# Sample attention: another order of the dilated mixer's far rows on the partitions

## What is computed

```python
DILATED_PATTERNS = ((128, 1), (512, 4), (2048, 16))
for window, dil in DILATED_PATTERNS:
    idx = n_buf + jnp.arange(T)[:, None] - dil * jnp.arange(window // dil + 1)[None, :]
    valid, idx = (idx >= 0), jnp.maximum(idx, 0)
    kg, vg = k_all[:, idx], v_all[:, idx]
    s = einsum('bthe,btjhe->bthj', q, kg) * scale
    p, lse = softmax_stats(s, valid);  o = einsum('bthj,btjhe->bthe', p, vg)
return merge_by_denominator(parts)
```

## Time and profile before

| | |
|---|---|
| Median of the runs | 2409.5 us |
| Profiled execution | 2408.45 us; 2406.9 us from its first to its last instruction |
| Granted TensorE clock, mean | 0.904 |
| TensorE busy (matmul) | 2074.7 us, 86% of the span |
| VectorE, ScalarE, GpSimd busy | 575.7, 379.6, 99.5 us |
| DMA | 537.21 MB in 287292 packets, mean 223 GB/s |
| Sample attention | from 254 to 637 us of the span |

### The profile page before, as it was taken

How to read it: one execution, slowest core, us unless ns; L and a number is a source line. 1 busy time by engine, 2 the same in 40 slices (tenths; PEclk the granted TensorE clock), 3 DMA queues, 4 the chain that set the end, 5 groups by cost and what they waited for, 6 DMA issues and landing times. The chain is left out here.

```text
span 2406.9 us, 52735 instructions
## 1 busy us (share of the span) xinstructions
PE 2074.7 (86%) x22761; PEld 1414.9 (59%) x22761; DVE 575.7 (24%) x1206; ACT 379.6 (16%) x924; POOL 99.5 (4%) x184
## 2 busy tenths in 40 slices
PE   6979488788789999889765786899999999999975
PEld 4755354355367777657443684566876666667643
DVE  2023254253210000112236623211112111111103
ACT  2014132232110000112001320210111011011101
POOL 0000111212100000000000000000000000000001
PEclk9989689889999999996886757899999999999987
DMA  7339699999843230554401011779897879889795
GB/s 269 105 133 337 205 258 321 282 290 321 282 161 140 87 141 1 184 164 169 125 16 30 12 36 57 286 281 347 331 350 285 321 280 376 327 336 406 294 409 174
DMA packets 287292, 537.21 MB, mean 223 GB/s; under 512 B 30021, under 2 KB 80130, under 8 KB 287068
## 3 DMA queue, kind: packets, MB, share of 16 engines
q1 hardware_dynamic: 273894, 492.37, 58.4%
q0 software_dynamic: 12960, 41.43, 5.0%
q10 hardware_dynamic: 214, 0.13, 0.0%
HBM read 520.44 MB, written 13.44 MB: 222 GB/s over the span
## 5 line engine op out<-in xcount | busy, mean ns | idle before, releaser
L2312 PE MATMUL PS<-moe_ring,moe_X 128*32 128x256 f32 (+1 forms) x5376 | 295.0, 369 | 20.8 <-DMA moe_ring<-in_moe_w 15.5
L415 PE MATMUL PS<-H,w_ring 128*128 128x320 f32 (+1 forms) x1008 | 282.0, 443 | 33.0 <-DMA w_ring<-in_w_in_odd 20.1
L2332 PE MATMUL PS<-moe_ring,moe_HT 128*32 128x256 f32 x4224 | 261.6, 382 | 3.6 <-issue 2.3
L415 PEld LDWEIGHTS PS<-H,w_ring 128*128 128x128 f32 (+1 forms) x1008 | 194.2, 194 | 117.2 <-DMA w_ring<-in_w_in_odd 20.4
L2312 PEld LDWEIGHTS PS<-moe_ring,moe_X 128*32 128x32 f32 x5376 | 185.5, 112 | 117.2 <-issue 20.2
L2312 PE MATMUL PS<-moe_ring,H 128*32 128x256 f32 (+1 forms) x3840 | 204.7, 362 | 4.7 <-issue 4.7
L1145 PE MATMUL PS<-H,ffn_ring 128*128 128x320 f32 x704 | 191.7, 436 | 3.5 <-ACT H L240 3.5
L833 PE MATMUL PS<-ident,KV 128*128 128x128 f32 x832 | 123.3, 313 | 72.9 <-DMA KV<-in_cache_win_kv 25.2
L2332 PEld LDWEIGHTS PS<-moe_ring,moe_HT 128*32 128x32 f32 x4224 | 148.0, 111 | 63.8 <-issue 7.1
L2312 PEld LDWEIGHTS PS<-moe_ring,H 128*32 128x32 f32 x3840 | 133.4, 110 | 65.2 <-issue 6.6
L1145 PEld LDWEIGHTS PS<-H,ffn_ring 128*128 128x128 f32 x704 | 134.9, 192 | 60.1 <-issue 4.8
(11 more groups left out here) (463 smaller groups left out, 1841.7 us busy)
## 6 DMA issues: line engine op xcount, KB each, us to landing
moe_ring<-in_moe_w SPq DMA_DIRECT2D x168, 1024.0 KB, 10.3
moe_ring<-in_moe_w SPq DMA_DIRECT2D x40, 2048.0 KB, 15.9
ada_ring<-in_ada_w SPq DMA_DIRECT2D x24, 2048.0 KB, 15.2
KV<-in_cache_win_kv SPq DMA_DIRECT2D x128, 256.0 KB, 9.0
KV<-in_cache_moba_kv POOLq DMA_DIRECT2D x128, 256.0 KB, 6.5
KV<-in_cache_moba_kv SPq DMA_DIRECT2D x128, 256.0 KB, 8.5
ffn_ring<-in_ffn_w SPq DMA_DIRECT2D x14, 2048.0 KB, 12.8
moe_ring<-in_moe_w SPq DMA_DIRECT2D x32, 512.0 KB, 8.4
```

What stands on the lines that cost most here:

```text
L415: last = pe.matmul(PS[0:width, banks[g % B], 0:TOK], RING[:, n % R, k, m:m + width], rhs[:, k, :], start=(k == 0), stop=(k == KT - 1))
L2312: mm = pe.matmul(PS[32 * j:32 * j + 32, i % 2, 0:2 * w].rearrange("p (a n) -> p a n", a=2), X[:, k, UNIT * u:UNIT * (u + 1)], RING[:, slot ...
L2332: mm = pe.matmul(PS[32 * g:32 * g + 32, 3, 0:256], HT[:, i % 2, 32 * j:32 * j + 32], rows[:, 256 * g:256 * (g + 1)], start=(j == 0), stop= ...
```

## The change

The far view names its dimensions in another order, the load takes the slice of eight rows on the outer one, and the host's table of row numbers follows:

```diff
-        far = io["cache_win_kv"][:, 0:FAR_TILES * 256].rearrange("b (i m r) a h e -> b a i m r (h e)", m=16, r=16)
+        far = io["cache_win_kv"][:, 0:FAR_TILES * 256].rearrange("b (i m r) a h e -> b a i r m (h e)", m=16, r=16)
...
-                                src = far[bass.ds(b, 1), kv, t, :, 0:8].rearrange("o m r n -> (o m) r n")
+                                src = far[bass.ds(b, 1), kv, t, 0:8].rearrange("o r m n -> (o r) m n")
...
-    rows = np.concatenate([16 * (far // 8) + far % 8, np.arange(FAR_TILES * 256, PAST)])
+    rows = np.concatenate([256 * (far // P) + 16 * (far % 16) + far % P // 16, np.arange(FAR_TILES * 256, PAST)])
```

## The result

The changed kernel takes 2485.2 us (median of 4 runs, 2477.9 to 2488.6) against 2407.6 us of before: the ratio is 1.0312, with a 95% interval from 1.0276 to 1.0348, or +75 us. The forecast was 2442 us, slower by 32 us. Direction, place and the number of engines were right and the time is inside the range; the price of a packet was not, and the size was off by more than a factor of two.

What follows compares the result with a forecast made beforehand. The prediction took TensorE, waiting on the window rows' transfer in the sample attention, as the bound: 2408.45 + 42 - 10 = 2440.5 us for the profiled execution, 2442 us as median, range 2407 to 2500 us.

Steps and rivals of the forecast that it cites:

- the range: Whole kernel: 2407 to 2500 us, leaving out the faster rival and the dearest part of the 2495 us rival.
- the price of a packet: Window loads on busy engines: 95 ns per far packet, 110 ns per near one, 202 us in all, +42 us.
- The bound: Sample attention: TensorE loses some 50 us to the window rows' transfer, so a longer transfer lengthens the kernel.
- 8 engines: Far tile loads: split along the source's outermost 8 rows, so 8 engines instead of 16, assumed always the same.
- The packets: Window rows, per busy engine: 96 x 16 + 512 = 2048 packets instead of 1280.
- The demand argument: Far loads: half of the engines demand at most 186 GB/s, under the tensor's 268, so packets get cheaper than 125 ns.
- The remainder: Window stretches: 160 of 183 us are packets; the rest goes to constants, GpSimd's pages and edges.
- What is hidden: Stretch from 313 to 356 us, TensorE busy nearly throughout: 10 of the 42 us taken to be hidden.
- The clock: TensorE after longer idle times: work may start at a slower clock, up to 8 us, left in the range.
- Rival 1: Far tiles on 8 engines with packets as dear as now, 125 ns: +86 us, 2495 us; chance 0.20.
- Rivals 3 and 4: Far loads: 3, faster by 16 or changing engines and cheaper order, 2386 us, 0.08; 4, no effect, 2409.5 us, 0.06.
- What would show it: Profile signs: 768 fewer packets, window share 0.6 to 0.75, 200 to 250 GB/s, first wait 22 to 27 us, pages 88 ns.

Runs made afterwards that it cites:

- the first probe: Kernel before plus an added phase of loads alone, 28 tiles of 256 KB per way of reading: far by group 27.9 us, far by row 54.9 us.
- The third probe: Kernel before plus an added phase issuing two bursts (48 DMAs, 10.5 MB) without slot waits: 41.2 us all by group, 62.6 us all by row.
- the mixed kernels: Kernel before with only some window tiles on 8 engines: 16 far +36 us, 48 far +66 us, 32 near in short steps +46 us.
- one_of_six: Kernel before with the new row order for one far tile of six (16 of 96 DMAs): ratio 1.0149, +36 us.
- half_tiles: Kernel before with the new row order for every second far tile (48 of 96 DMAs): ratio 1.0273, +66 us.
- the second probe: Kernel before plus an added phase of page-tensor loads with varied row steps: on 8 engines 88 to 90 ns a packet, 122 in the changed kernel's order.

## Why the prediction was right or wrong

- *The bound.* Right. The loss is mostly in TensorE's waits for window rows and for the copy behind the constants; the other engines did the same work.
- *8 engines.* Right, to the packet: 286524. The reading of 26 landings in the earlier trace rows gave it, and the probe adds what no row of before showed: from SyncE they are the same 8 each time. The Trainium skill's rule (DMA: Bandwidth & Descriptors, "Why a DMA increments its semaphore by 16 and not by 1"), the divisor of both sides and the lowest-numbered engines, agrees with the 768 packets and with the share of 0.50; which numbers they have no run shows.
- *The packets.* Right: 2048 instead of 1280 on the busy engines.
- *The price of a packet.* This is the step that failed. I took 95 ns for the far packets and 110 for the near ones, because half of the engines ask for less than the tensor can give. The demand argument was wrong for this order: by row a packet costs 122 ns on 8 engines in the first probe, not 88 to 97, though only 134 GB/s are moved. The third probe has the term in full: 62.6 us for 512 packets is 122 ns, and four times 62.6 - 41.2 us is +86 us in place of my +42. That a mix of transfers on 8 and on 16 engines has a price of its own I had not thought of either, but by the sum above it explains the mixed kernels and not the change.
- *The remainder.* Of the 183 us of window stretches I put 160 to packets at 125 ns and held 23 for fixed. The measured stretches are 183 / 1280 = 143 ns a packet before, and in one_of_six (26 + 49 + 50 + 50 + 26) / 1408 = 143 again, but 222 / 1664 = 133 in half_tiles and 236 / 2048 = 115 in the changed kernel, where the busy engines still work off window packets in the page stretches. So these stretches do not tell fixed time from price.
- *What is hidden.* I let 10 us disappear in the stretch where TensorE was busy. This failed too. That stretch grew from 43 to 59 us, more than any other, and the +86 of the phase is the probe's +86, so nothing is seen to be hidden there.
- *The clock.* Left in the range with up to 8 us; TensorE's busy time in the phase rose by 15.8 us with the clock at 0.81, about twice the 8 us of the range; how much of this reached the end is not shown, since TensorE waits for rows beside it.
- *Rival 1* (+96 us raw, +86 in the end, 2495 us), with 0.20, was nearest to the truth by its price, though its reason, a latency that belongs to the tensor, is wrong: near tiles of the same tensor take 93 ns alone. Its price of a packet stayed, 123 ns against 126 in the third probe. Rivals 3 and 4 fell with the packet count, and the hope of rival 3 for a better order with the second probe, where neighbouring engines on neighbouring rows take 16 x 2048 x 0.96 / 225 = 140 ns on 16 engines.
- *What would show it.* The rate fell to 197 to 228 GB/s, near the 200 to 250 foreseen, but the share only to 0.76 to 0.86 where 0.6 to 0.75 had been named, the wait behind the constants rose to 29 us where it was 22 to 27, and the page stretches did not keep their price: 96 to 98 ns in three of them, against 91 to 94 before. The page stretches growing by 25 us was not foreseen; the busy engines' backlog reaches into them by the order of the queue, which is argued and not shown.
- *The range.* By the same sum 91 and 112 ns for the far packets give +26 and +58 us, +66 with the clock's 8; the +18 of the forecast has no working.

## What to carry to other kernels

Give a DMA an outermost dimension that is a multiple of 16 on both sides (here a source of 8 was enough to halve the engines, with 128 on the other side); count the landings in the packet line to see what it got. Sixteen transfers on half of the engines among 176 on all of them cost 36 us, over twice their own 16 x 8 packets at 125 ns, so the last few are worth mending too. And price a transfer by a stretch that reads in that order, on that many engines, in that mix: a 2 KB packet took from 88 to 142 ns on SyncE's queue here. For the full change the plain product did: packets on the busiest engine times the price of that order.

## What the runs showed of the hardware that was not expected

- From SyncE's queue on 8 engines a 2 KB packet takes 122 ns where the source is 8 rows 4 KB apart (outermost) by 16 rows 64 KB apart, 116 ns with 32 KB for the 64, and 89 ns with 68 KB.
- 128 consecutive rows come at 93 to 95 ns from either tensor, while 16 groups of 8 rows out of 16 come at 115 to 124 ns, at 64 or 384 KB between the groups, and at 110 with 68 KB.
- The same source with 8 outermost gives a DMA share of 0.50 from SyncE's queue and 0.88 from GpSimd's, at 134 and 190 GB/s, and GpSimd's has 64 small packets more for each such DMA.
